# Hybrid attention: eight units taken up in another order by three interleaved slots

## Chip, cores and metric

The kernel runs on one core of a Trainium2 chip. The metric is the device time of one execution in microseconds (us), taken as the median of several executions. The engines are TensorE (PE), VectorE (DVE), ScalarE (ACT), GpSimd (POOL) and SyncE (SP), each with its own queue that is worked through in the written order.

## The reference

A first block of two layers (neighbourhood attention and a bidirectional RWKV-7 mixer, each followed by a mixture of experts) is followed by a second block of two hybrid layers. The change is in the hybrid layers. Each of them projects 512 tokens and runs four branches side by side; two of them, called sparse and stick here, are attentions with 4 heads of 64, in blocks of 128 queries:

```
def dsa_sparse_attention(q, k, v, iq, ik, iw):
    ...
    logits = jnp.where(valid[:, None], logits, neg)
    probs = jax.nn.softmax(logits, axis=-1)
    return jnp.einsum('bhqk,bqkhd->bqhd', probs.astype(v.dtype), v_sel)

def stick_breaking_attention(q, k, v):
    ...
    log_beta = jax.nn.log_sigmoid(z)
    log_keep = jnp.where(strict, jax.nn.log_sigmoid(-z), 0.0)
    after = lax.cumsum(log_keep, axis=3, reverse=True) - log_keep
    wts = jnp.where(strict, jnp.exp(log_beta + after), 0.0)
    return jnp.einsum('bhqs,bshd->bqhd', wts.astype(v.dtype), v)
...
o = jnp.stack([o_a, o_b, o_c, o_d], axis=2)
o = o * jax.nn.silu(gate_paths.reshape(B, S, N_BRANCHES, BRANCH_WIDTH))
```

The outputs of the eight blocks (two kinds, four query blocks) don't depend on one another, nor do they depend on the order in which they are computed.

## The kernel before

The program is a list of stages; in each stage every engine has a function that issues its instructions in order, with waits on counting semaphores. At a stage's end all engines are awaited (`fence`). A hybrid layer has the stages `h_norm`, `h_mix` (projections, rotary, the selection of keys as an additive mask), `h_attend` (L3619), `h_merge` and `h_out`. The layer runs twice, so `h_attend` runs twice.

`h_attend` works on eight units: kind stick or sparse, and a query block `bq` of 0 to 3. Below, "stick 3" is the stick unit with `bq` 3. Since attention is causal, a unit of block `bq` has W = 128 (bq + 1) keys; for its four heads together an elementwise instruction covers 4W elements per partition, so 2048 for block 3 and 512 for block 0. A stick unit has 12 steps, a sparse unit 6. Three slots hold a unit each, in three buffers that the profile names `oT` (slot 0), `big` (slot 1) and `c` (slot 2, a tile of the weight ring, whose other tiles are named `c` too). `attend_order` (L3598) writes out the order: it goes round the slots, and in each call a slot does one step of its unit; a slot whose unit has ended takes up the next of the list `units`. There are 72 such calls, the same list for all engines.

The steps of a stick unit: scores (step 0: PE, with ACT copying them out of PSUM), absolute value and exponential (1, ACT), add 1 (2, DVE), logarithm (3, ACT), maximum-and-add (4, DVE), mask of the diagonal block (5, POOL), four scans and a subtraction (6, DVE), exponential (7, ACT), mask (8, POOL), turns of the weights (9, PE, copied out by ACT for heads 0 and 2 and by DVE for heads 1 and 3), output products (10, PE, with `tok`), copy of the output (11, ACT). The steps of a sparse unit: scores (0, PE, with DVE scaling and masking them out of PSUM), maximum (1, DVE), four exponentials with sums (2, ACT), turns (3, PE), output products (4, PE, with `aV`), scaling of the output (5, DVE).

Between these steps stands other work: in each call, up to the 64th, PE issues one of the 64 products of the gate (`product`, two matmuls of 128x512 each, `ps<-c,hT`). Every eighth call completes a gate tile; then ACT takes its tanh and DVE forms the gate's product with it (`turned`, `weighed`). So when a unit's result is not there yet, PE has at most the products that stand before the step in the order. PSUM has eight banks, handed out in turn: scores, turned weights, outputs and gate tiles take them, and the next one to take a bank waits until its reader has let it go.

ACT's exponential and tanh share a table set; the logarithm has another, and a table load stands in the program where the set changes.

```
X, k0 = (fc, 2) if stick else (qkT, 2)
...
if step == (9 if stick else 3):
    e.wait_ge(*(P.pool if stick else P.act).at(*k_('weights', u)))
```

The scores of stick units read `fc`, those of sparse units `qkT`.

Of the kernel before, what the change touches and what calls it, by code (L numbers as in the profile page):

```python
# [3596 lines left out]

def attend_order():  # L3598

    units = [(kind, bq) for bq in (3, 2, 1, 0) for kind in ('stick', 'sparse')]  # L3600
    steps = {'stick': 12, 'sparse': 6}
    active, last, order, n = {}, {}, [], 0
    while n < 8 or active:
        for s in range(3):
            if s not in active and n < 8:
                active[s] = [n, last.get(s), 0]
                last[s] = n
                n += 1
            if s in active:
                u, before, step = active[s]  # L3610
                kind, bq = units[u]
                order.append((u, kind, bq, s, before, step))
                active[s][2] += 1
                if step + 1 == steps[kind]:
                    del active[s]
    return order, units, last


def h_attend(P, I, l, k_, ring, hT, oT, o, aV, qkT, big, fc, tok, madd):  # L3619
    d = ExitStack()  # L3620
    order, units, last = attend_order()
    ones = P.sb([128, 512], name="ones", ctx=d)
    st = P.sb([128, 4, 3, 4], name="ast", ctx=d)
# [561 lines left out]
```

How the kernel before makes its waits and increments, by code:

```python
    def wait_ge(self, sem, value):  # L53
        if self.e is not None and value > self.made.get(id(sem), 0):
            self.made[id(sem)] = value
            self.e.wait_ge(sem, value)
# [112 lines left out]
    def fetch(self, e, i, src, k=8, n=512):  # L169
        for f in self.free(i):
            e.wait_ge(*f)
        e.dma_start(self.tile(i, k, n), src.rearrange("(k p) n -> p k n", p=128)).then_inc(*self.sig[i % self.n].inc('load', id(self), i))
# [29 lines left out]
    def act(self, e, m):  # L202
        ks = slice(2 * m, 2 * m + 2)
        e.wait_ge(*self.ring.loaded(self.i))
        for f in self.ring.free(self.j):
            e.wait_ge(*f)
        e.activation(self.high[:, ks], self.raw[:, ks], ACT.Copy).then_inc(*self.P.act.inc('high', m, *self.name))
# [1 line left out]
    def lower(self, e, m, by):  # L210
        ks = slice(2 * m, 2 * m + 2)
        e.wait_ge(*self.P.act.at('high', m, *self.name))
        e.tensor_tensor(self.low[:, ks], self.raw[:, ks], self.high[:, ks].bitcast(F32), SUB).then_inc(*by.inc('low', m, *self.name))
# [10 lines left out]
    def pe(self, e, out, high, low, *lows):  # L224
        for k in range(8):
            e.wait_ge(*self.P.act.at('high', k // 2, *self.name))
            e.matmul(out, high(k), self.high[:, k], k == 0, False)
        for k in range(8):
            e.wait_ge(*self.lowered(k // 2))
            e.matmul(out, high(k), self.low[:, k], False, False)
        for s, *event in lows:
            e.wait_ge(*s.at(*event))
        for k in range(8):
            ins = e.matmul(out, low(k), self.high[:, k], False, k == 7)
        return ins
```

## Time and profile before

| | us |
|---|---|
| median of 3 runs | 4246.2 |
| lowest and highest | 4231.04, 4247.58 |
| profiled execution | 4249.68 |
| its span | 4248.0 |
| attention stage, first hybrid layer | from 3069.2 to 3182.3 of the span |
| attention stage, second hybrid layer | from 3740.8 to 3854.6 |

The span is the time between the first and the last instruction of the profiled execution; the execution's own time is 1.7 us longer. A row in order of time gives start, duration, engine, source line, operation, output and inputs, shape, how many instructions are merged, and in brackets how long the engine stood idle before it and what ended that. The source lines are those of small helpers (L62 is every matmul, L66 every turn, L72 every activation, L81 every three-operand DVE instruction), so one goes by the tiles' names. Matmuls overlap, so a row's duration contains a tail; the time that a piece of work takes from PE is the distance from its start to the start of the next row. A gate product is two matmuls, since f32 goes in two passes: a row with x16 is eight products.

### The profile page before, as it was taken

The page shows a single profiled execution, that of the slowest core. Times are in us where ns is not written, and L with a number is a line of the kernel's source. Part 1 is how long each engine was busy: PE and PEld are TensorE (multiplying, and loading weights), DVE is VectorE, ACT ScalarE, POOL GpSimd, SP SyncE. Part 2 cuts the span into 40 slices and gives each one's busy share as a digit, 9 for nine tenths or more (in the row PEclk, how much of TensorE's full clock was granted, in tenths as well). Part 3 has the DMA queues.
Part 4 walks back from the last instruction along what each step waited for, and adds up shares of the span by engine and source line. Part 5 has one row for each costly group of instructions (what it writes and reads, how often), then busy time and mean ns, then how long its engine had stood idle before and what let it go on. Part 6 is the DMA issues. An engine that isn't in the chain of part 4 may idle for free.

```text
span 4248.0 us, 60025 instructions
## 1 busy us (share of the span) xinstructions
PE 3768.5 (89%) x26061; PEld 2364.1 (56%) x26061; DVE 1732.7 (41%) x3103; ACT 1224.7 (29%) x2255; POOL 462.0 (11%) x503
## 2 busy tenths in 40 slices
PE   6999979999989985488898798888989998989998
PEld 5777763433435444377786432235756755756764
DVE  3326531212242256745635312225853324854322
ACT  3226431111122266443342210003252212334211
POOL 2211020000000122210012100000102200101210
PEclk9999989999999987667898899999999999989999
DMA  7521219898863149833341599994203220212221
GB/s 250 179 77 46 83 76 365 322 368 321 321 266 117 59 147 315 246 88 99 97 128 62 216 400 420 420 420 155 80 33 122 84 104 21 80 60 85 104 89 40
DMA packets 311064, 739.21 MB, mean 174 GB/s; under 512 B 67928, under 2 KB 144224, under 8 KB 261648
## 3 DMA queue, kind: packets, MB, share of 16 engines
q1 hardware_dynamic: 299296, 697.93, 44.6%
q0 software_dynamic: 11504, 37.44, 2.6%
q8 instruction: 205, 3.36, 0.3%
q14 instruction: 59, 0.48, 0.0%
HBM read 673.41 MB, written 61.89 MB: 173 GB/s over the span
## 4 chain that ended last, share of the span: by engine, by line
PE 73%; DMA 10%; DVE 9%; ACT 4%; issue 1%; POOL 1%; SPq 0%; DVEq 0%; POOLq 0%; ACTq 0%
PE ps L62 70%; DMA raw<-in_moe_w_dram 7%; PE ps L66 4%; DMA b<-in_ada_w_dram 2%; DVE mx L75 1%; DVE spr L75 1%; DVE o L75 1%; DVE sT L75 1%; DMA sa<-Ad 0%; DVE b L75 0%; ACT TZ L72 0%; ACT c L72 0%; DMA c<-in_w_in_dram 0%; ACT b L72 0%; DVE cr L75 0%
## 5 line engine op out<-in xcount | busy, mean ns | idle before, releaser
L62 PE MATMUL ps<-raw,xinT 128*64 128x512 f32 (+1 forms) x4096 | 596.0, 494 | 45.1 <-DMA raw<-in_moe_w_dram 36.5
L62 PEld LDWEIGHTS ps<-raw,xinT 128*64 128x64 f32 (+1 forms) x4096 | 195.5, 124 | 426.0 <-issue 291.6
L62 PE MATMUL ps<-wp,hp 128*128 128x512 f32 x1536 | 360.8, 396 | 11.0 <-DVE wp L75 11.0
L62 PEld LDWEIGHTS ps<-wp,hp 128*128 128x128 f32 x1536 | 291.1, 190 | 78.1 <-DVE wp L75 11.4
L62 PE MATMUL ps<-raw,hidT 128*64 128x512 f32 x1024 | 241.2, 606 | 13.5 <-DMA raw<-in_moe_w_dram 13.5
L62 PE MATMUL ps<-c,hT 128*128 128x512 f32 x512 | 234.0, 608 | 3.6 <-issue 2.2
L62 PE MATMUL ps<-c,oT 128*128 128x512 f32 x512 | 222.8, 592 | 1.4 <-ACT oT L72 1.4
L62 PE MATMUL ps<-xr,b 128*128 128x512 f32 (+1 forms) x432 | 161.2, 533 | 9.2 <-ACT xr L72 4.6
L75 DVE TENSOR_TENSOR mx<-mx,ps 128x512 f32<-128x512 f32 x156 | 105.2, 685 | 156.4 <-PE ps L62 156.2
L75 DVE TENSOR_TENSOR wp<-c,wp 128x1536 fp32r<-128x1536 f32 x32 | 58.4, 1824 | 261.8 <-ACT wp L72 261.8
L62 PE MATMUL ps<-ar,naxh 128*128 128x512 f32 x576 | 147.6, 406 | 19.2 <-DVE ar L75 8.8
L62 PEld LDWEIGHTS ps<-c,oT 128*128 128x128 f32 x512 | 97.0, 190 | 117.0 <-issue 111.0
L62 PEld LDWEIGHTS ps<-c,hT 128*128 128x128 f32 x512 | 95.8, 194 | 115.9 <-issue 113.6
L72 ACT ACTIVATE hidT<-ps 128x512 f32<-128x512 f32 x32 | 19.1, 597 | 453.6 <-PE ps L66 453.6
L62 PEld LDWEIGHTS ps<-raw,hidT 128*64 128x64 f32 x1024 | 67.5, 138 | 144.4 <-issue 110.5
L72 ACT ACTIVATE wp<-c 128x2048 fp32r<-128x2048 f32 x32 | 61.2, 1911 | 290.0 <-PE ps L62 290.0
L75 DVE TENSOR_TENSOR hid<-hid,ps 128x512 f32<-128x512 f32 x64 | 44.0, 687 | 234.6 <-ACT hid L72 212.5
L62 PEld LDWEIGHTS ps<-ar,naxh 128*128 128x128 f32 x576 | 108.2, 193 | 49.1 <-DVE ar L75 10.5
L62 PEld LDWEIGHTS ps<-xr,b 128*128 128x128 f32 x432 | 82.4, 193 | 86.9 <-issue 71.0
L75 POOL TENSOR_TENSOR wp<-c,wp 128x512 fp32r<-128x512 f32 x32 | 85.5, 2673 | 349.3 <-ACT wp L72 326.6
L62 PE MATMUL ps<-cr,or 128*128 128x512 f32 (+2 forms) x512 | 110.7, 370 | 14.2 <-ACT or L72 14.1
L62 PEld LDWEIGHTS ps<-cr,or 128*128 128x128 f32 x512 | 91.3, 197 | 27.0 <-issue 14.6
(502 smaller groups left out, 6402.5 us busy)
## 6 DMA issues: line engine op xcount, KB each, us to landing
raw<-in_moe_w_dram SPq DMA_DIRECT2D x384, 1024.0 KB, 9.3
c<-in_w_in_dram SPq DMA_DIRECT2D x28, 2048.0 KB, 7.9
mx<-in_ada_w_dram SPq DMA_DIRECT2D x14, 2048.0 KB, 7.9
b<-in_ada_w_dram SPq DMA_DIRECT2D x8, 2048.0 KB, 10.3
a<-in_na_w_qkv_dram SPq DMA_DIRECT2D x6, 2048.0 KB, 8.0
c<-in_w_branch_dram SPq DMA_DIRECT2D x16, 512.0 KB, 4.0
c<-in_w_out_dram SPq DMA_DIRECT2D x4, 2048.0 KB, 8.5
c<-in_w_ple_gate_dram SPq DMA_DIRECT2D x4, 2048.0 KB, 7.6
```

What stands on the lines that cost most here:

```text
L62: return self.e.matmul(out, lhsT, rhs, start=start, stop=stop, skip_group_check=True) if self.e is not None else self
L66: return self.e.transpose(out, in_, ident[0:k, 0:k]) if self.e is not None else self
L72: return self.e.activation(*a, **k) if self.e is not None else self
L75: return self.e.tensor_tensor(*a, **k) if self.e is not None else self
```

## The change

The list of units is replaced by another, in which the three largest stick units come first:

```diff
-    units = [(kind, bq) for bq in (3, 2, 1, 0) for kind in ('stick', 'sparse')]
+    units = [('stick', 3), ('stick', 2), ('stick', 1), ('sparse', 3), ('stick', 0), ('sparse', 2), ('sparse', 1), ('sparse', 0)]
```

Before, the slots held: slot 0 stick 3, then stick 1; slot 1 sparse 3, 2, 1, 0 one after the other; slot 2 stick 2, then stick 0. Now: slot 0 stick 3, then sparse 3, then sparse 1; slot 1 stick 2, then stick 0; slot 2 stick 1, then sparse 2, then sparse 0. Both orders have 24 rounds of three calls.

What PE issues at the start of the stage, before:

```order
L62 MATMUL ps<-fc 128x512 x4
L62 MATMUL ps<-c,hT 128x512
L62 MATMUL ps<-qkT 128x512 x4
L62 MATMUL ps<-c,hT 128x512
L62 MATMUL ps<-fc 128x384 x4
L62 MATMUL ps<-c,hT 128x512 x8
L66 MATMUL ps<-ident,big 128x128 x16
L62 MATMUL ps<-c,hT 128x512 x3
L62 MATMUL ps<-aV,big 128x64 x16
L62 MATMUL ps<-c,hT 128x512 x6
L62 MATMUL ps<-qkT 128x384 x4
L62 MATMUL ps<-c,hT 128x512 x8
```

and now:

```order
L62 MATMUL ps<-fc 128x512 x4
L62 MATMUL ps<-c,hT 128x512
L62 MATMUL ps<-fc 128x384 x4
L62 MATMUL ps<-c,hT 128x512
L62 MATMUL ps<-fc 128x256 x4
L62 MATMUL ps<-c,hT 128x512 x25
L66 MATMUL ps<-ident,oT 128x128 x16
L62 MATMUL ps<-c,hT 128x512
L66 MATMUL ps<-ident,big 128x128 x12
```

The first turns of the stage are now those of stick 3 (`oT`), behind 25 gate products in a row; before, sparse 3's turns (`big`) stood behind eight. (Here a gate product counts once.)

What DVE issues at the start of the stage, up to the subtraction of stick 3, before:

```order
L81 SCALAR_TENSOR_TENSOR big<-ps,mx 128x512 x4
L93 TENSOR_REDUCE ast<-big 128x4
L78 TENSOR_SCALAR oT<-oT 128x2048
L81 SCALAR_TENSOR_TENSOR c<-c,ps 128x512
L78 TENSOR_SCALAR c<-c 128x4x384
L96 RECIPROCAL ast<-ast 128x4
L90 COPY big<-ps 128x512 x2
L81 SCALAR_TENSOR_TENSOR oT<-oT 128x2048
L81 SCALAR_TENSOR_TENSOR c<-c 128x4x384
L81 SCALAR_TENSOR_TENSOR c<-c,ps 128x512
```

and now:

```order
L78 TENSOR_SCALAR oT<-oT 128x2048
L81 SCALAR_TENSOR_TENSOR c<-c,ps 128x512
L78 TENSOR_SCALAR big<-big 128x4x384
L78 TENSOR_SCALAR c<-c 128x4x256
L81 SCALAR_TENSOR_TENSOR oT<-oT 128x2048
L81 SCALAR_TENSOR_TENSOR big<-big 128x4x384
L81 SCALAR_TENSOR_TENSOR c<-c 128x4x256
L81 SCALAR_TENSOR_TENSOR c<-c,ps 128x512
L84 SCALAR_TENSOR_TENSOR oT<-ones,oT 128x512 x4
L75 TENSOR_TENSOR oT<-oT 128x2048
L84 SCALAR_TENSOR_TENSOR big<-ones,big 128x384 x4
L75 TENSOR_TENSOR big<-big 128x4x384
```

The sparse unit's score additions, maximum, reciprocal and copies are gone from here, and the third stick unit's add and maximum-and-add have come in (L84 are the scans, `c<-c,ps` the gate's product).

What ACT issues for stick 0, sparse 3 and sparse 2 in the second half of the stage, now:

```order
L72 ACTIVATE big<-big 128x4x128 x2
L72 ACTIVATE oT,ast<-oT,ast 128x512 x4
L72 ACTIVATE c,ast<-c,ast 128x384 x4
L72 ACTIVATE oT<-ps 128x512 x2
L72 ACT_TABLE_LOAD
L72 ACTIVATE big<-big 128x4x128
L72 ACT_TABLE_LOAD
L72 ACTIVATE c<-ps 128x512
L72 ACTIVATE c<-ps 128x384 x2
```

The eighth row is the gate's tanh; before it now stand two units' exponentials, a logarithm and two table loads. ACT has five table loads in the stage, before it had seven.

## Rows read from the trace of the kernel before

**Rows 1.** The page, busy time of the busiest engine: busy us (share), instructions

```profile
PE 3768.5 (89%) x26061; PEld 2364.1 (56%) x26061; DVE 1732.7 (41%) x3103; ACT 1224.7 (29%) x2255; POOL 462.0 (11%) x503
```

**Rows 2.** Stretches, the attention stage's two runs: busy per engine, PEclk, DMA share

```profile
3069.00:3182.00 113.00, 101.20 (x432) 59.29 (x432) 54.97 (x81) 55.46 (x99) 7.54 (x9) 0.92 0.07 24
...
3740.00:3855.00 115.00, 101.97 (x432) 59.57 (x432) 55.87 (x84) 56.21 (x100) 7.54 (x9) 0.92 0.07 24
```

**Rows 3.** PE in order of time, first layer; the last row, second layer

```profile
3069.23 2.05 PE L62 MATMUL ps<-c,hT 128*128 128x512 f32 x2 [1.10 <-issue]
3071.21 2.87 PE L62 MATMUL ps<-fc 64*128 64x512 f32 x8
3074.01 1.12 PE L62 MATMUL ps<-c,hT 128*128 128x512 f32 x2
3075.07 1.99 PE L62 MATMUL ps<-qkT 64*128 64x512 f32 x8
...
3078.04 1.56 PE L62 MATMUL ps<-fc 64*128 64x384 f32 x8
3079.53 7.13 PE L62 MATMUL ps<-c,hT 128*128 128x512 f32 x16
3092.18 3.68 PE L66 MATMUL ps<-ident,big 128*128 128x128 f32 x16 [5.51 <-ACT big L72]
...
3122.70 1.97 PE L66 MATMUL ps<-ident,oT 128*128 128x128 f32 x8 [5.53 <-DVE c L81]
...
3145.42 1.14 PE L62 MATMUL ps<-fc 64*128 64x256 f32 x8
...
3177.31 0.33 PE L66 MATMUL ps<-ident,big 128*128 128x128 f32 x1 [0.21 <-DVE c L81]
...
3732.61 7.06 PE L62 MATMUL ps<-tok,ws 128*128 128x64 f32 x32 [3.81 <-POOL bn L78]
```

**Rows 4.** Stretches as in rows 2, behind PE's stalls: the eighth figure is PEclk

```profile
3092.10:3096.50 4.40, 4.32 (x18) 3.81 (x18) 1.48 (x4) 4.37 (x6) 0.00 (x0) 0.50 0.00 0
3096.50:3117.00 20.50, 20.50 (x82) 11.32 (x80) 15.93 (x17) 5.47 (x5) 3.83 (x3) 0.99 0.00 1
...
3736.00:3740.00 4.00, 3.67 (x18) 3.48 (x17) 3.39 (x16) 0.00 (x0) 0.00 (x0) 0.50 0.00 0
```

**Rows 5.** ACT in order of time, first layer

```profile
3080.66 1.91 ACT L72 ACTIVATE oT<-oT 128x2048 f32<-128x2048 f32 x1
3082.59 1.28 ACT L72 ACT_TABLE_LOAD   x1
3083.88 1.91 ACT L72 ACTIVATE oT<-oT 128x2048 f32<-128x2048 f32 x1
3085.82 3.00 ACT L72 ACTIVATE c<-c 128x1536 f32<-128x1536 f32 x2
...
3089.21 0.71 ACT L72 ACTIVATE big<-big,ast 128x512 f32<-128x512 f32 x1
...
3152.09 2.15 ACT L72 ACTIVATE oT<-oT 128x1024 f32<-128x1024 f32 x2
```

**Rows 6.** DVE in order of time, first layer

```profile
3078.85 2.29 DVE L93 TENSOR_REDUCE ast<-big 128x4 f32<-128x2048 f32 x1
...
3098.70 1.75 DVE L81 SCALAR_TENSOR_TENSOR c<-c 128x1536 f32<-128x1536 f32 x1
...
3105.92 4.56 DVE L84 TENSOR_TENSOR_SCAN oT<-ones,oT 128x512 f32<-128x512 f32 x4
3110.52 2.29 DVE L75 TENSOR_TENSOR oT<-oT 128x2048 f32<-128x2048 f32 x1
...
3114.59 3.88 DVE L84 TENSOR_TENSOR_SCAN c<-ones,c 128x384 f32<-128x384 f32 x4
```

**Rows 7.** POOL in order of time, first layer: the masks of stick 3

```profile
3098.86 2.10 POOL L114 TENSOR_SCALAR_AFFINE_SELECT oT<-oT 128x512 f32<-128x512 f32 x1 [29.20 <-DVE oT L81]
...
3114.82 1.15 POOL L114 TENSOR_SCALAR_AFFINE_SELECT oT<-oT 128x512 f32<-128x512 f32 x1 [13.28 <-ACT oT L72]
```

## Prediction

> **What bounds the kernel now.** Five views were read, from the coarse to the fine. The page's busy times [rows 1] show TensorE (PE) busy for 89% of the span: only time in which it stands, or runs at the lower clock, can move much. The change touches one stage, the hybrid layers' attention, which runs twice; the table of stretches [rows 2] gives each run about 113 us (115 with the edges taken wider), with PE busy for 101.2 us of 113 and DVE and ACT for half. The whole stage is 2 x 113 = 226 us of 4248, and PE's matmuls in it are the same in number and shape before and after. What can change is how long PE stands there and how long its clock is low afterwards.
>
> PE's order of time [rows 3] shows where it stands: 5.51 us before the turns (transposes) of sparse unit 3 (`big`), 5.53 us in the middle of the turns of stick unit 3 (`oT`), 0.21 us near the end; 11.25 us in all. Between these it runs back to back. The clock table [rows 4] shows what follows a stall: 0.50 of full speed, the 1.2 GHz level, for the 4.4 us behind the first one, then 0.99, the 2.4 GHz level. In those 4.4 us PE did 2.2 us of full-clock work, so such a stall costs 2.2 us more. Together the stage has 11.25 + 2 x 2.2 = 15.7 us to give, 31 us in two runs. A measurement of this kernel can tell about 0.5%, 21 us, from no change.
>
> **How a unit's chain runs.** Before its turns a stick unit needs: ACT's copy of its scores out of PSUM, absolute value, a table load, exponential; DVE's add of 1; ACT's logarithm; DVE's maximum-and-add; POOL's mask; four scans and a subtraction on DVE; ACT's exponential; POOL's mask. Each engine takes its instructions in the written order, so a unit's step also waits for what the other two slots have put ahead of it.
>
> **Term 1, the wait for stick 3's weights.** Before the change PE stops at sparse 3's turns and again at stick 3's. Now the first three units are all stick units, and PE has 25 products of the gate in a row behind their scores. PE's arrival [rows 3]: the scores of 512 keys end at 3074.01; then product 1.06 (from 3074.01 to the next row's start, 3075.07), scores of 384 keys 1.49 (3078.04 to 3079.53), product 1.06, scores of 256 keys 1.06 (the row's 1.14 less such an overlap), which makes 3078.7. The 25 products follow; eight of them took 7.13 us with the last one's tail of 0.25, so 0.86 each, 21.7 in all with the 0.2 that the first one takes more: **3100.4**.
>
> The chain, with durations from [rows 5, 6]: the third unit's scores end at 3078.7, ACT's last copy of them 0.9 later (before, the 384-key scores ended at 3079.53 and ACT was through with their copies at 3080.66; these are shorter): 3079.6. Absolute value, load and exponential of 128x2048 took from 3080.66 to 3085.8, 5.1 us: 3084.7. The pair for 128x1536, 3.0, and for 128x1024, 2.15: 3089.9. The gate's tanh 0.6 (by size, from the same rows), a load 1.3, the logarithm of 128x2048 1.9: 3093.7. DVE's maximum-and-add of 128x2048 about 2.3 (1.75 for 128x1536), the second unit's 1.75, the third's 1.2 by size, the gate's product 0.7: 3099.5. Four scans of 128x512, 4.56: 3104.1. Subtraction 2.29: 3106.4. ACT's exponential 1.9 and POOL's mask, 1.15 beside a scan [rows 7], with handovers of 0.1 to 0.2: **3109.7**. Before, the subtraction ended at 3112.8: the sparse unit's 2.5 + 2.3 us of DVE work and its 2.9 us on ACT (four times 0.71) are out of the way, but the third stick unit's are in it. So PE stands 3109.7 - 3100.4 = **9.3 us** once, where it stood 5.51 and 5.53.
>
> **Term 2, the next two units.** DVE goes on with the second unit's scans, 3.88, and its subtraction, 1.75, and the third's, 2.7 and 1.2 by size, before it copies any turned weights out of PSUM; the exponentials go through ACT in the same order. PE's next turns need those banks and those weights. The same addition, carried on row by row, gives waits of 0.5, 1.6 and 0.8, **2.9 us**. First half: 12.2.
>
> **Term 3, the second half.** Sparse 3 and sparse 2 now start together, beside stick 0. Take the start of sparse 3's scores as zero. PE: scores 1.9, product 1.06, scores of 128 keys 0.6 by size, product 1.06, scores of 384 keys 1.5, seven products 6.2: it wants sparse 3's turns at 12.4. DVE ends sparse 2's score additions at about 7.3 and the gate's product (behind a tanh, behind the third of these products) at 8.9; only then comes the maximum over sparse 3, 2.3, then ACT's 2.9: 14.1. A wait of **1.7**. Then ACT has sparse 2's exponentials (2.4), two copies (1.1), a table load (1.3), stick 0's logarithm (0.6), a load (1.3) and only then the tanh (0.6) on which DVE's next gate product (0.7) waits, whose bank the fourth head of sparse 2 needs: 22.2. PE, through sparse 3's turns, two products and nine turns, is there at 18.7: **3.5 us**. The small units at the end give 0.7 (a bank for sparse 0's scores) and 2.0 (a bank behind the exponentials of sparse 1 and 0). That is 7.9 in the second half, where [rows 3] has 0.21.
>
> **The sum.** The whole addition, every instruction at its row's duration and each engine in its written order, gives 20.3 us of waits and 120.5 us for the stage now. The same addition for the order before gives 13.2 and 113.3, against 11.25 and 113.1 by the rows [rows 2, 3]: it makes the waits a little long and PE's own work a little short, and the total right. So +7.1 us in each run. PE's own work: 0. The half clock: two stalls long enough before (5.5 each), two now (9.3 and 3.5): 0. Table loads: seven before, five now, 2 x 1.28 us less of ACT, worth nothing, since the two removed stood where PE had products; two of those left are in the 3.5 us wait. SP's queue has the same list; its one load behind the stage is released by sparse 0 instead of stick 0, both at the very end. Sum: 2 x 7.1 = **+14 us**. The profiled execution took 4249.7 us (span 4248.0), 3.5 above the median of 4246.2; I put the sum on the median: **4260 us**.
>
> Bounds for one run of the stage: below, if each of the eight waits is 0.3 too long and the 3.5 us stall leaves the clock up, 7.1 - 2.4 - 2.2 = +2.5. Above, if POOL's masks take the 2.10 us of [rows 7] each time, 0.5 more, +7.6. The clock behind the second stall is the larger unknown; it is the first rival.
>
> A table load took 1.28 us, and the next exponential began 1.29 us after the load did [rows 5]. The Trainium skill (ScalarE: Activation LUTs, section "What ACT_TABLE_LOAD costs") counts a drain of 1.38 us on top, 2.66 us for a switch. By that rule the 3.5 us wait would be 2.8 us longer and the sum 20 instead of 14; the trace does not show the drain, and the measurement decides.
>
> **The rivals.** Rival 1, slower by more than 0.5%: PE's clock stays low through the sparse pair. In the second layer there is a stall of 3.81 us, after which 32 matmuls of 64 columns took 7.06 us, with 0.50 granted up to 3740 though PE had no gap [rows 3, 4]. Behind my 3.5 us stall stands the same kind: three turns, a product, 16 output products of 64 columns, two products, 12 more, 9.1 us of full-clock work. All at half clock it costs 9.1 us, not the 2.2 of the forecast: +14.0 a run, 4274. It decides for "slower" from 3.5 us a run onwards, 4267. For it: that row. Against: in the first layer the clock came back after 4.4 us, though with 128-column turns and full products.
>
> Rival 2, about even: the waits of the second half don't come, because banks and tanh meet PE more kindly than I read them. Then 12.2 + 0.5 of waits against 13.2, and one fall of the clock less: -2.7 a run, 4241. Against: the steps of term 3 stand end to end, with no slack of 1.7 us.
>
> Rival 3, faster by over 0.5%: the 25 products hide stick 3's chain altogether, and the rest follows without a wait. All 15.7 us a run would go, 4215. For it: 21.7 us of products is the longest unbroken cover that the stage has had. Against: the chain of term 1 has no gap between 3080 and 3106 that could close.
>
> **How the numbers follow.** Forecast 0.62, rival 1 0.24, rival 2 0.10, rival 3 0.04. Forecast and rival 2 lie within 0.5% (4225 to 4267): 0.72; rival 1 is slower, 0.24; rival 3 faster, 0.04. The range goes from rival 2's 4241 to 4276, which is rival 1's price and a little for the spread of the runs (4231 to 4248).
>
> **What would show it.** Right: about 120 us for the stage in both layers; one stall of some 9 us before the turns of `oT` in place of two of 5.5; a stall before the fourth head of sparse 2, ended by DVE's gate product; five table loads. Wrong: a first stall under 6 us (term 1), no stall over 2 us in the second half (term 3), or a granted clock of 0.5 for more than 5 us behind the second stall (rival 1). A change of time outside the two stages would be against the whole argument.

## The result, and the profile after

| | before | after |
|---|---|---|
| median | 4240.9 us (20 runs) | 4255.8 us (20 runs) |
| lowest and highest | 4231.0, 4249.7 | 4242.7, 4267.1 |
| ratio to before, 95% interval | | 1.0034 (1.0025 to 1.0042) |
| span of the profiled execution | 4248.0 | 4246.9 |
| attention, first layer | 113.95 us | 118.70 us |
| attention, second layer | 114.71 us | 125.49 us |

The change makes the kernel 0.34% slower, 14.4 us by the ratio (14.9 between the medians), within the 0.5% that was called no change; with twenty runs on either side the difference is clear of noise. A stage is measured here from the start of its first gate product to the start of the first turn of the merge (`ident,o`), because that is what the next stage waits for; this is 0.9 us more than the forecast's 113.1.

The span of the profiled execution after the change is a little shorter than that of before, although its two stages are 15.5 us longer. The first stage begins at 3054.45 instead of 3069.23: work in front of it, which the change does not touch, took 14.8 us less in this execution. Single executions of one and the same kernel lie up to 19 us (before) and 24 us (after) apart. So one must compare stages here, and the medians of many runs, never two spans.

PE in order of time, kernel after, first layer (the rows of before are [rows 3]):

```profile
3054.45 2.04 PE L62 MATMUL ps<-c,hT 128*128 128x512 f32 x2 [1.10 <-issue]
...
3063.89 21.73 PE L62 MATMUL ps<-c,hT 128*128 128x512 f32 x50
3095.30 3.68 PE L66 MATMUL ps<-ident,oT 128*128 128x128 f32 x16 [9.68 <-POOL oT L114]
...
3102.53 0.55 PE L66 MATMUL ps<-ident,big 128*128 128x128 f32 x3 [1.52 <-DVE c L81]
3103.50 0.55 PE L66 MATMUL ps<-ident,big 128*128 128x128 f32 x3 [0.43 <-ACT oT L72]
...
3133.75 1.97 PE L66 MATMUL ps<-ident,oT 128*128 128x128 f32 x16 [1.54 <-ACT oT L72]
...
3141.68 0.55 PE L66 MATMUL ps<-ident,c 128*128 128x128 f32 x3 [3.26 <-DVE c L81]
3142.06 1.02 PE L62 MATMUL ps<-c,hT 128*128 128x512 f32 x2
3142.92 3.68 PE L62 MATMUL ps<-aV,oT 128*128 128x64 f32 x32
...
3158.02 0.71 PE L62 MATMUL ps<-qkT 64*128 64x128 f32 x8 [0.55 <-DVE c L81]
...
3166.93 0.44 PE L66 MATMUL ps<-ident,oT 128*128 128x128 f32 x2 [1.33 <-DVE c L81]
```

The reader sees the forecast's list of waits in the forecast's places: 9.68 behind 25 products (50 matmuls), then 1.52 and 0.43, then in the second half 1.54, 3.26, 0.55 and 1.33. They sum to 18.31 us, where [rows 3] has 11.25: 7.06 us more. The same waits stand in the second layer, to 0.01 us. What follows the 3.3 us wait differs:

```profile
3816.90 0.90 PE L66 MATMUL ps<-ident,c 128*128 128x128 f32 x3 [3.27 <-DVE c L81]
3817.59 1.91 PE L62 MATMUL ps<-c,hT 128*128 128x512 f32 x2
3819.30 6.92 PE L62 MATMUL ps<-aV,oT 128*128 128x64 f32 x32
3826.02 3.73 PE L62 MATMUL ps<-c,hT 128*128 128x512 f32 x4
```

The 32 output matmuls took 6.72 us to the next row's start, in the first layer 3.52. The stretches behind PE's waits, with PEclk as the eighth figure (first layer, two stretches; second layer, three):

```profile
3095.20:3099.60 4.40, 4.30 (x18) 3.81 (x18) 4.37 (x6) 1.72 (x2) 0.21 (x2) 0.54 0.00 0
3141.60:3146.00 4.40, 4.32 (x34) 3.84 (x34) 1.71 (x5) 0.07 (x1) 0.64 (x1) 1.00 0.01 2
3816.80:3821.00 4.20, 4.10 (x14) 3.06 (x14) 1.73 (x5) 0.09 (x1) 0.63 (x1) 0.50 0.02 4
3821.00:3825.00 4.00, 4.00 (x21) 4.00 (x20) 0.00 (x0) 0.00 (x0) 0.00 (x0) 0.50 0.00 0
3825.00:3829.40 4.40, 4.40 (x10) 2.47 (x10) 0.42 (x1) 0.00 (x0) 0.00 (x0) 0.50 0.00 0
```

In the first layer the clock is at 2.4 GHz (1.00) behind the wait; in the second, behind the same wait, at 1.2 GHz (0.50) for 12.6 us, although PE is busy without a gap. From PE's turn at this wait to the stage's end it is 31.47 us in the first layer and 37.64 in the second: 6.2 of the 6.8 us between 118.70 and 125.49. The other 0.6 lies at the stage's start, where stick 3's scores (`ps<-fc`, x8) took 3.41 us to the next row's start instead of 2.81.

Why the 3.3 us wait is there, from ACT in order of time, first layer:

```profile
3136.00 1.06 ACT L72 ACTIVATE oT<-ps 128x512 f32<-128x512 f32 x2
3137.07 1.28 ACT L72 ACT_TABLE_LOAD   x1
3138.37 0.63 ACT L72 ACTIVATE big<-big 128x512 f32<-128x512 f32 x1
3139.01 1.28 ACT L72 ACT_TABLE_LOAD   x1
3140.31 1.36 ACT L72 ACTIVATE c<-ps 128x512 f32<-128x512 f32 x3
```

Load, logarithm of stick 0, load, and only then the tanh (the first of the three merged rows); DVE's gate product follows at 3140.94 and PE's turn at 3141.68.

And why the first wait is 9.7 us, from ACT (three rows out of a stretch without a gap) and then from DVE:

```profile
3066.73 1.28 ACT L72 ACT_TABLE_LOAD   x1
...
3075.65 1.28 ACT L72 ACT_TABLE_LOAD   x1
3076.95 1.91 ACT L72 ACTIVATE oT<-oT 128x2048 f32<-128x2048 f32 x1
```

```profile
3078.89 2.29 DVE L81 SCALAR_TENSOR_TENSOR oT<-oT 128x2048 f32<-128x2048 f32 x1 [1.06 <-ACT oT L72]
3081.10 1.75 DVE L81 SCALAR_TENSOR_TENSOR big<-big 128x1536 f32<-128x1536 f32 x1
3082.77 1.66 DVE L81 SCALAR_TENSOR_TENSOR c<-c 128x1024 f32<-128x1024 f32 x1
3084.35 0.67 DVE L81 SCALAR_TENSOR_TENSOR c<-c,ps 128x512 f32<-128x512 f32 x1
3084.95 4.98 DVE L84 TENSOR_TENSOR_SCAN oT<-ones,oT 128x512 f32<-128x512 f32 x4
3089.96 2.29 DVE L75 TENSOR_TENSOR oT<-oT 128x2048 f32<-128x2048 f32 x1
```

The chain has two parts. ACT works without a gap from 3064.81 to the end of stick 3's logarithm, 3078.86: absolute values and exponentials of all three sticks, a tanh and two table loads. DVE had waited 1.06 us for that logarithm. From then on DVE has no idle time to the end of the subtraction, 3092.2, since stick 3's scans stand behind the maximum-and-add of all three sticks. ACT's exponential and POOL's mask end the chain at 3095.2. PE had run out of products at 3085.6.

### The profile page after: what moved, and what is told of

The parts are those of the page before. It is cut to its first block, busy times and chain, and to the rows that moved or that the text cites. A ratio compares the mean times of both kernels' runs of the same rounds, so it can differ in the third digit from the quotient of the medians.

```text
span 4246.9 us, 60023 instructions
## 1 busy us (share of the span) xinstructions
PE 3764.2 (89%) x26061; PEld 2362.7 (56%) x26061; DVE 1730.5 (41%) x3103; ACT 1218.6 (29%) x2251; POOL 463.7 (11%) x503
## 4 chain that ended last, share of the span: by engine, by line
PE 72%; DMA 10%; DVE 9%; ACT 5%; issue 1%; POOL 1%; SPq 0%; DVEq 0%; POOLq 0%; ACTq 0%
PE ps L62 69%; DMA raw<-in_moe_w_dram 7%; PE ps L66 3%; DMA b<-in_ada_w_dram 1%; DVE mx L75 1%; ACT oT L72 1%; DVE o L75 1%; DVE spr L75 1%; ACT c L72 1%; DVE sT L75 0%; DMA sa<-Ad 0%; DVE cr L75 0%; SPq L120 0%; ACT TZ L72 0%; ACT b L72 0%
## 5 line engine op out<-in xcount | busy, mean ns | idle before, releaser
L62 PE MATMUL ps<-raw,hidT 128*64 128x512 f32 x1024 | 242.4, 610 | 12.6 <-DMA raw<-in_moe_w_dram 12.6
```

The costliest lines, as they stand in the source:

```text
L62: return self.e.matmul(out, lhsT, rhs, start=start, stop=stop, skip_group_check=True) if self.e is not None else self
```

## The experiments

All time ratios are to the kernel before, run on the same chip; stages are given first layer, second layer. `ln_later`, `fill_stall` and `scan1` edit the changed kernel; the other orders replace its list of units.

**The changed kernel once more.** No edit.

> The changed kernel itself once more, for its clock behind the stall of 3.3 us in the second half of each attention stage. In the profiled execution that stall left the clock at 2.4 GHz in the first layer (stage 117.8 us) and at 1.2 GHz for some 12 us in the second (stage 124.6 us). Theory A (whether the clock falls is open from one execution to the next, and worth about 6 us a stage): the time is 1.003 to 1.0045 of before, with a wider spread of the single times than the kernel before has, and the profile shows either case in either layer. Rival (it belongs to the layer: the second layer comes into the stage at a low clock, the first not): the profile shows again 118 and 125 us, the clock up in the first layer and down in the second.

Measured: 1.0034 (1.0022 to 1.0046), 4255.8 us against 4241.6. Stages 124.99 and 118.85. This time the clock fell in the first layer and stayed up in the second, the other way round:

```profile
3148.00:3152.40 4.40, 1.21 (x10) 0.91 (x8) 0.67 (x2) 4.36 (x6) 0.00 (x0) 0.87 0.00 0
3152.40:3157.00 4.60, 4.53 (x16) 3.50 (x16) 1.71 (x5) 0.06 (x1) 0.64 (x1) 0.50 0.01 2
3157.00:3165.00 8.00, 8.00 (x27) 6.05 (x27) 0.42 (x1) 0.00 (x0) 0.00 (x0) 0.51 0.00 0
```

So it does not belong to the layer: the same wait of 3.26 us, in the same place of the same kernel, lets the clock fall in one execution and not in the next. A wider spread was expected too: 22 us lie between lowest and highest in 11 runs here, 23 in 27 of before; the standard deviations are 7.3 and 4.6 us. With the `scan1` profile below, it fell in three of six stages. It costs 6.0 to 6.2 us, by the time from the wait's end to the stage's end in the three executions. The Trainium skill (TensorE: Matmul & The Clock Gate, Part 1) says that how many matmuls run at the low clock varies from one run to another of the same kernel. The trace agrees: here it is 6 us in one stage and nothing in the other, behind the same wait.

**The logarithm one call later.** In `act` of `h_attend`:

```diff
-                if step == 3:
+                if step == 4:
                     e.wait_ge(*P.dve.at(*k_('plus', u)))
                     e.activation(Sw, Sw, ACT.Ln).then_inc(*P.act.inc(*k_('ln', u)))
```

> The logarithm of a stick unit is issued by ACT one call later, behind the gate's tanh instead of ahead of it; nothing else moves in the first half. Theory A (the 3.3 us stall before sparse 2's fourth head is ACT's table load, logarithm and second load ahead of the tanh on which the bank waits): the two loads and the logarithm, 3.2 us, leave the way, the stall shrinks from 3.3 to under 1 us, the clock never falls there, and the time lies 2 x (2.7 to 5) us below the changed kernel: 4246 to 4251 where the changed kernel has 4256. Rival (the stall is the exponentials of both sparse units, 5.3 us on ACT, and the loads only fill time): the stall stays above 2.5 us and the time at 4256.

Measured: 1.0010 (1.0000 to 1.0021), 4247.4 us. Stages 115.85 and 116.10. ACT now, and PE's row at the same turn:

```profile
3135.18 1.47 ACT L72 ACTIVATE c<-ps 128x512 f32<-128x512 f32 x3 [0.42 <-PE ps L62]
3136.67 1.28 ACT L72 ACT_TABLE_LOAD   x1
```

```profile
3136.55 0.55 PE L66 MATMUL ps<-ident,c 128*128 128x128 f32 x3 [0.43 <-DVE c L81]
```

The tanh comes ahead of the loads, the wait falls from 3.26 to 0.43, and 2.8 us less of it brings 2.8 us in a stage whose clock had stayed up (118.70 to 115.85) and 9.4 in one whose clock had fallen. The rival, under which the exponentials alone made the wait, is out. The Trainium skill (ScalarE: Activation LUTs, section "What ACT_TABLE_LOAD costs") counts 2.66 us for each switch of tables; by that the wait would have been about 6 us, an estimate (3.26 and twice 1.38). The logarithm started 1.30 us after its load did (3137.07 to 3138.37), so the trace disagrees with that rule.

**The wait filled with work.** PE repeats a turn, whose result it writes again into its own bank, before it signals:

```diff
-def pe_turns(P, e, key, sources, *emptied):
+def pe_turns(P, e, key, sources, *emptied, again=0):
...
+    for _ in range(again):
+        e.turn(P.psum[0:sources[0].shape[1], b, 0:sources[0].shape[0]], sources[0], P.ident)
     for j, s in enumerate(sources):
...
-                             (P.dve if hh % 2 else P.act,) + k_('wT', u, hh))
+                             (P.dve if hh % 2 else P.act,) + k_('wT', u, hh), again=24 if (kind, bq, hh) == ('sparse', 2, 2) else 0)
```

> PE turns sparse 2's third head 24 times more before it signals that head, which puts 2.6 us of full-clock work into the 3.3 us stall; results are unchanged and the stall's cause too. Theory A (part of the change's cost is the clock that falls behind this stall in some executions): the clock stays at 2.4 GHz in both layers, the stage is about 118 us in both, and the time lies below the changed kernel by the average of that loss, 2 to 7 us: 4249 to 4254. Rival (the clock's fall is not worth anything on average, or falls for another reason): the same time as the changed kernel, 4256, or up to 2 us more.

Measured: 1.0021 (1.0012 to 1.0031), 4251.4 us, against 4255.8 of the changed kernel on the same chip. Stages 119.02 and 118.54. PE in order of time, and the granted clock behind it:

```profile
3138.38 3.77 PE L66 MATMUL ps<-ident,c 128*128 128x128 f32 x33
3142.79 0.55 PE L66 MATMUL ps<-ident,c 128*128 128x128 f32 x3 [0.64 <-DVE c L81]
```

```profile
3143.00:3147.00 4.00, 4.00 (x33) 3.52 (x31) 1.42 (x3) 0.00 (x0) 0.63 (x1) 1.00 0.01 2
3147.00:3155.00 8.00, 8.00 (x42) 5.38 (x42) 0.85 (x2) 0.00 (x0) 0.00 (x0) 1.00 0.01 2
```

The turn comes at the same point as before, since its cause is elsewhere; 24 useless turns cost nothing that can be measured (119.02 and 118.54 against 118.70 and 118.85 with the clock up), and the clock stayed up in both layers. Two stages could show that by chance, about one time in four if it falls in half of them. The spread of the times speaks for it as well: their standard deviation is 4.3 us here, 7.3 in the changed kernel's eleven runs and 4.6 in before's. The intervals of the two ratios overlap (from 1.0022 to 1.0031), so the 4.4 us between the medians are not clear of the noise by themselves, and only a rough measure of what the falling clock costs on average. Two stages at 6.1 us each, in half of the cases, would be 6.1; the 4.4 say a third of the cases. The other part of the loss is what remains, 8.9 us by the stages (119.02 + 118.54 less 113.95 + 114.71), and 1.0021 is 8.9 us.

**One scan instead of four for stick 3.** Left out: the running sums of three of stick 3's four heads.

```diff
-                    for hh in G4:
+                    for hh in (G4 if bq < 3 else (0,)):
                         e.tensor_tensor_scan(B[:, 4 + hh, 0:W][:, ::-1], ones[:, 0:W], B[:, 4 + hh, 0:W][:, ::-1], 0.0, MUL, ADD).then_inc(*P.dve.inc())
```

> The changed kernel with one of stick 3's four scans on DVE, the first head's; the other three heads' running sums are left out, everything else stands. Theory A (the 9.7 us stall before stick 3's turns is set by DVE's in-order chain to stick 3's weights): three scans of 1.14 us leave the way, the first stall goes from 9.7 to 6.3 us and the stage is 3.4 us shorter, apart from the clock behind the 3.3 us stall. Rival (ACT, with its table loads and three units' exponentials, sets it): the stall stays above 9 us.

Measured in one run: 4253.4 us, no ratio. Stages 115.58 and 122.05; behind the 3.3 us wait the clock stayed up in the first layer and fell in the second. DVE and PE, first layer:

```profile
3096.25 1.64 DVE L84 TENSOR_TENSOR_SCAN oT<-ones,oT 128x512 f32<-128x512 f32 x1
```

```profile
3103.27 3.68 PE L66 MATMUL ps<-ident,oT 128*128 128x128 f32 x16 [6.34 <-POOL oT L114]
```

The scans went from 4.98 us to 1.64, the wait from 9.68 to 6.34: 3.34 us of DVE's work, 3.34 of PE's wait. So DVE's in-order chain is on the path to the first wait, us for us, and the rival's prediction of a wait above 9 us fails. ACT's part is not excluded by this: its exponentials and loads stand on the same path, ahead of DVE's part (the rows above, to 3078.86), and no run took them away.

**The three sticks first, another second half.**

Against the changed kernel:

```diff
-    units = [('stick', 3), ('stick', 2), ('stick', 1), ('sparse', 3), ('stick', 0), ('sparse', 2), ('sparse', 1), ('sparse', 0)]
+    units = [('stick', 3), ('stick', 2), ('stick', 1), ('sparse', 2), ('sparse', 3), ('stick', 0), ('sparse', 0), ('sparse', 1)]
```

> The three sticks first, as in the change, but behind them sparse 2, sparse 3, stick 0, sparse 0, sparse 1, so that stick 0's logarithm is not ahead of the tanh. Theory A (the change costs about as much in the first half as the old order did, 11.7 against 11.2 us of waits, and its loss stands in the second half): first half unchanged (9.7, 1.5, 0.4), second half under 3.5 us of waits with none above 1.5, stage about 113 to 114 us from its start to the merge's first turn, time within 0.15% of before (4235 to 4248). Rival (the three sticks side by side are what costs): at least 0.25% above before, 4252 or more.

Measured: 1.0000 (0.9984 to 1.0015), 4241.8 us against 4241.0. Stages 114.73 and 115.19. The first half's waits are unchanged (9.70, 1.52, 0.43), the second half's are 0.59, 0.43, 0.78 and 0.32. The stages are 0.7 and 1.2 us above the 113 to 114 expected; the time lies where it was expected. So an order that begins with the three large sticks can be as fast as the old one; the 14 us hang on the order of the units behind them.

**One stick beside two sparse units.** Two orders, found by the forecast's addition of rows:

```diff
+    units = [('sparse', 2), ('sparse', 3), ('stick', 2), ('sparse', 0), ('stick', 3), ('stick', 1), ('stick', 0), ('sparse', 1)]
```

> Another order of the eight units: sparse 2, sparse 3, stick 2, sparse 0, stick 3, stick 1, stick 0, sparse 1, so that a long stick chain has short sparse units beside it and PE comes to short chains first. Theory A (PE's waits come from how many long chains stand side by side on DVE and ACT, and an addition of the rows tells which order has few): the stage is about 101 us with no stall over 2 us, that is 12 to 13 us a stage less than the kernel before, 25 us in all: ratio to before 0.993 to 0.995, 4213 to 4222. Rival (the waits come with the amount of DVE and ACT work, and another order only moves them): a stage of 110 to 120 us, ratio to before 0.998 to 1.004.

Measured: 0.9937 (0.9924 to 0.9949), 4216.5 us. Stages 101.60 and 102.03. PE, first layer, all the rows with a wait between the stage's first product and its end:

```profile
3084.41 0.55 PE L66 MATMUL ps<-ident,oT 128*128 128x128 f32 x3 [1.65 <-ACT oT L72]
3085.61 1.20 PE L66 MATMUL ps<-ident,oT 128*128 128x128 f32 x9 [0.66 <-DVE c L81]
...
3115.04 0.66 PE L66 MATMUL ps<-ident,oT 128*128 128x128 f32 x4 [1.56 <-ACT oT L72]
```

3.87 us of waits instead of 11.25, and the half-clock stretches behind the two long ones gone: 12.4 and 12.7 us a stage, 25 in all; the time fell by 25.1 between the medians, 26.7 by the ratio. This version beats both kernels.

The heading holds for the first six rounds only. By the list, stick 3 then stands beside stick 2 for six rounds, and beside the small sticks 1 and 0 for six more. What the order avoids is that two of the sticks 3, 2 and 1 start in the same round, as they do before (3 and 2), after (3, 2 and 1) and in `late_sticks` below (2 and 1, with 0). No run separates the offset starts from the early sparse units here.

```diff
+    units = [('sparse', 2), ('sparse', 3), ('stick', 3), ('sparse', 0), ('stick', 2), ('stick', 1), ('stick', 0), ('sparse', 1)]
```

> As the order with one stick at a time, but with stick 3 first and stick 2 later: sparse 2, sparse 3, stick 3, sparse 0, stick 2, stick 1, stick 0, sparse 1. Theory A (what counts is that one long chain stands beside two short ones, whichever stick it is): stage 102 to 103 us, 0.993 to 0.995 of before, the same as the other order within 0.1%. Rival (the gain of the other order came from putting stick 3 off until later): stage 108 us or more, ratio 0.997 or more.

Measured: 0.9945 (0.9927 to 0.9964), 4219.7 us. Stages 104.24 and 104.27. The order of the two large sticks matters little, 2.4 us a stage: the first wait is 2.72 us instead of 1.65, and behind it the clock dipped (the eighth figure of the second row):

```profile
3082.00:3086.40 4.40, 1.68 (x4) 0.38 (x2) 0.00 (x0) 4.39 (x11) 0.00 (x0) 1.00 0.00 0
3086.40:3091.00 4.60, 3.94 (x15) 2.57 (x16) 3.00 (x6) 4.00 (x11) 0.00 (x0) 0.68 0.00 0
```

The stage is over a microsecond above the 102 to 103 expected, which reckoned with no fall there.

**The sticks bunched at the end.**

```diff
+    units = [('sparse', 3), ('sparse', 2), ('stick', 3), ('sparse', 1), ('sparse', 0), ('stick', 2), ('stick', 1), ('stick', 0)]
```

> Sparse 3, sparse 2 and stick 3 first, then sparse 1 and 0, and the sticks 2, 1 and 0 side by side at the end. Theory A (long chains side by side make waits wherever they stand, and at the end the gate's products run out): few waits at first (under 4 us until stick 3's turns), then some 4 and 5 us before the last sticks' turns, stage about 115 to 118 us, ratio to before 1.000 to 1.006. Rival (sparse units at the start are all that matters): stage 102 to 106 us, ratio 0.993 to 0.996.

Measured: 1.0058 (1.0039 to 1.0077), 4268.8 us against 4241.0. Stages 125.60 and 126.09. PE from the second long wait on, first layer:

```profile
3108.84 1.97 PE L66 MATMUL ps<-ident,oT 128*128 128x128 f32 x8 [4.46 <-ACT oT L72]
...
3114.23 1.91 PE L66 MATMUL ps<-ident,c 128*128 128x128 f32 x16
...
3134.50 21.73 PE L62 MATMUL ps<-c,hT 128*128 128x512 f32 x50
3161.31 2.80 PE L66 MATMUL ps<-ident,oT 128*128 128x128 f32 x12 [5.09 <-POOL oT L114]
3165.49 0.88 PE L66 MATMUL ps<-ident,big 128*128 128x128 f32 x6 [1.38 <-POOL big L114]
3167.90 0.44 PE L66 MATMUL ps<-ident,big 128*128 128x128 f32 x2 [1.53 <-ACT oT L72]
...
3169.10 5.22 PE L62 MATMUL ps<-tok,oT 128*128 128x64 f32 x24
```

The expected waits came in part only. Before stick 3's turns (`ident,c`, 3114.23) under 4 us were expected and 8.15 measured: 3.15 and 0.54 at sparse 3's turns and 4.46 at sparse 1's. At the last sticks, 4 and 5 were expected, and 5.09, 1.38 and 1.53 came. With two sparse units first this is the slowest order tried: what comes first does not decide. The stage is 8 us above the 115 to 118 expected: besides the waits, the clock was low behind each of the three long ones (0.63 and 0.50 over 4.4 us; 0.50 from 3169 to the end), and 24 output matmuls took 5.02 us to the next row's start, at full clock 2.63. The ratio lies at the upper end of what was expected, 1.0058 against 1.006.

## Why the prediction was right

The time of 4260 stands against 4255.8 measured, or +14 against +14.4 us by the ratio on before's median; most of the difference between 4260 and 4255.8 comes from the three runs of before, whose median was 4246.2 where twenty give 4240.9. The waits, which make up the whole of the forecast's +14, came within 0.04 us a stage. That the time agreed as well is partly luck: the step on the clock was wrong twice, once in each direction. By its steps:

- **Term 1, the wait for stick 3's weights.** 9.3 forecast, 9.68 measured. PE's arrival (31.2 us into the stage) and the end of stick 3's logarithm (24.4) came as forecast. DVE's part took 13.4 us instead of 12.7: its `c` row 1.66 for 1.2, the scans 4.98 for 4.56. `scan1` shows that DVE's part is on the path; ACT's share in front of it is read from the trace alone. In this half the change trades two waits of 5.5 for one of 9.7 and two small ones.
- **Term 2.** 0.5, 1.6 and 0.8 forecast; 1.52 and 0.43 measured, the first did not come.
- **Term 3.** 1.7, 3.5, 0.7 and 2.0 forecast; 1.54, 3.26, 0.55 and 1.33 measured. The two table loads and the logarithm in the largest of them are shown by `ln_later`.
- **The sum of the waits.** The addition gave 13.2 before and 20.3 after (the terms as written add up to 20.1), measured 11.25 and 18.31: both 2.0 too long, so the difference, 7.1, came out at 7.06. An addition of this kind is to be read as a difference of two orders; here its error was common to both.
- **"The half clock: 0."** This step was wrong in both of its parts, and they nearly cancelled. The forecast held that two falls of the clock stand before and two after, each worth 2.2. Behind the waits of the first half it falls once instead of twice: where it stays up behind the 3.3 us wait, the stage is only 4.75 us longer in the first layer (118.70 - 113.95) and 4.14 in the second (`after_again`, 118.85 - 114.71) for 7.06 of waits, so 2.3 and 2.9 less. The 3.3 us wait lets it fall in some executions, and then for 12.6 us instead of 4.4, 6.0 to 6.2 us a time. The sum is an estimate: 8.9 us of fixed part, and 4.4 (`fill_stall`, not clear of the noise) to 6.1 (three of six stages) on average for the falling clock, 13 to 15 together. How often it falls in the median run was not measured.
- **The stage and its bounds.** Forecast was about 120 us in both layers, against 113.1. In that measure it was 117.8 in one and 124.6 in the other, and 124.1 and 118.0 in `after_again`: 120.5 is near the average of two cases, and neither case came out so. The bounds for one run of the stage, +2.5 to +7.6, hold for the stages with the clock up (+4.75) and not for those where it fell (+10.8, and +11.0 in `after_again`). The forecast's own third sign of being wrong, a granted clock of 0.5 for more than 5 us behind the second stall, did come, in half of the stages.
- **Rival 1** had the right mechanism and two thirds of its size right: it said 9.1 us for a fall that lasts through the output products. The low clock ended sooner than it said, after 12.6 us, and cost 6.0 to 6.2. Its fault was the place in the argument: it was given a chance as something that happens or not in the kernel, and it happens or not in each stage of each execution. An average over both cases is what the median sees.
- **Rival 2** (the second half without its waits) is what two edits come near to: `ln_later`, which takes away the largest of the four (1.0010), and `order_second`, whose four sum to 2.1 us (1.0000). **Rival 3** did not come: the 9.7 us wait stood in both orders that begin with the three sticks side by side.

The range held, and the spread of single runs (4243 to 4267) lies within it; its upper end, rival 1's price, was not reached.

## What to carry to other kernels

Where engines take their steps in one written order, and a result is wanted by the busiest engine, lay the units out so that long chains do not start together and have short ones beside them, and look for the slow step that stands ahead of an unrelated short one whose bank or buffer is waited for. A wait of the bounding engine is priced by its length and by what the clock does behind it, and where narrow matmuls follow, the second can be twice the first (3.26 and 6.1 us here). Add up rows for the old order too: the sum's error dropped out of the difference here, and the same addition found two faster orders. What it does not see is the clock, one reason why the sticks bunched at the end came out 8 us a stage above the forecast.

## What was not expected of the hardware

Behind a wait of 3.26 us the granted clock of TensorE fell to 1.2 GHz in three of six stages and stayed at 2.4 GHz in the other three, with identical instructions and waits equal to 0.01 us. Behind 2.72 us it dipped too, in both stages (mean 0.68 and 0.69 over 4.6 us), and behind 3.15 us in both stages of `late_sticks` (0.63 and 0.66 over 4.4 us); behind the 1.54 us wait the 16 turns ran at full speed (1.80 us to the next row's start, 3.47 behind the 9.68 us wait). Once low behind the 3.26 us wait, it stayed low for 12.6 us while PE was busy without a gap, through 3 turns, a product, 32 matmuls of 64 columns and two more products; behind the 9.68 us wait it was back within about 4.4 us, after 16 turns and a product. What in that work decides how soon it returns was not tried. POOL's first mask again took 2.09 us beside DVE's two-input instructions, where five later masks of the same size took 0.63 or 0.64. DVE's `c` row beside it took 1.66 us where its size would make it 1.2, and the four scans 4.98 where [rows 6] has 4.56. Both of these stand in DVE's unbroken chain, so by estimate 0.8 us of the 9.7 us wait are theirs.
